# Feed-forward by groups of four output tiles with 512-column matmuls, the left-over sums turned by VectorE and placed by DMAs within SBUF

## What is computed

```python
def conv_ffn(h, buf, w_up, w_gate, conv_w, conv_b, w_down):
    L = h.shape[1]
    up = h @ w_up
    gate = h @ w_gate
    ext = jnp.concatenate([buf.astype(gate.dtype), gate], 1)
    act = jax.nn.gelu(causal_dwconv(ext, conv_w, L) + conv_b)
    return (act * up) @ w_down, ext[:, -(FFN_CONV - 1):]
# in trunk: x = x + y (mixer); x = x + conv_ffn(rms_norm(x), ...); at the end rms_norm(x)
```

## Time and profile before

| | us |
|---|---|
| median of 3 runs (lowest, highest) | 2825.76 (2825.66, 2826.88) |
| profiled execution: device time | 2826.28 |
| profiled execution: span from first to last instruction | 2824.5 |
| TensorE busy | 2805.3 |
| VectorE busy | 1555.3 |
| ScalarE busy | 1032.5 |
| GpSimd busy | 123.6 |

### The profile page before, as it was taken

One profiled execution on the slowest core, in us unless ns is written; L12 is line 12 of the kernel. 1 busy time (PEld: TensorE's weight loads), 2 busy tenths in 40 slices (PEclk: granted clock), 3 DMA queues, 4 the chain that ended last, 5 costly groups with the idle time before them and its releaser, 6 DMA issues.

```text
span 2824.5 us, 49617 instructions
## 1 busy us (share of the span) xinstructions
PE 2805.3 (99%) x19055; PEld 2791.5 (99%) x19055; DVE 1555.3 (55%) x2178; ACT 1032.5 (37%) x1135; POOL 123.6 (4%) x136
## 2 busy tenths in 40 slices
PE   9999999999999999999999999999999999999998
PEld 8999999999999999999999999999999999999998
DVE  7666645554355544555666666455554455535554
ACT  5443333333333333333444444443333333333333
POOL 0000021000000000002200000220000000000012
PEclk9999999999999999999999999999999999999999
DMA  6444344444444444444444444444444444444443
GB/s 237 145 145 137 129 149 149 151 148 151 151 149 144 155 150 149 142 155 149 144 146 151 136 143 142 154 147 151 148 150 149 149 149 149 149 149 149 149 149 114
DMA packets 120784, 420.26 MB, mean 149 GB/s; under 512 B 13688, under 2 KB 19840, under 8 KB 120576
## 3 DMA queue, kind: packets, MB, share of 16 engines
q1 hardware_dynamic: 120128, 418.45, 44.7%
q10 hardware_dynamic: 576, 0.66, 0.1%
HBM read 412.92 MB, written 6.14 MB: 148 GB/s over the span
## 4 chain that ended last, share of the span: by engine, by line
PE 98%; DVE 1%; DMA 0%; ACT 0%; issue 0%; DVEq 0%; ACTq 0%
PE gb L463 95%; PE ab L469 3%; PE ab L482 1%; DMA x<-in_x 0%; DVE w_lo L1097 0%; PE ab L663 0%; DVE work L1731 0%; DVE work L1225 0%; DVE rt L1727 0%; DVE work L1189 0%; ACT w_hi L785 0%; DVE a_lo L1104 0%; DVEq L140 0%; ACT work L862 0%; ACTq L850 0%
## 5 line engine op out<-in xcount | busy, mean ns | idle before, releaser
L1097 DVE TENSOR_TENSOR w_lo<-raw,w_hi 128x1024 fp32r<-128x1024 f32 x767 | 943.4, 1230 | 1175.5 <-ACT w_hi L785 1173.5
L785 ACT ACTIVATE w_hi<-raw 128x1024 fp32r<-128x1024 f32 x769 | 814.5, 1060 | 1653.8 <-PE gb L463 1651.4
L463 PE MATMUL gb<-a_hi,w_hi 128*128 128x320 f32 x4216 | 1311.1, 311 | 0.5 <-DVE w_lo L1097 0.3
L463 PE MATMUL gb<-a_hi,w_lo 128*128 128x320 f32 x4216 | 1302.8, 309 | 0.0
L463 PE MATMUL gb<-a_lo,w_hi 128*128 128x320 f32 x4216 | 1302.7, 309 | 0.0
L463 PEld LDWEIGHTS gb<-a_hi,w_hi 128*128 128x128 f32 x4216 | 791.6, 188 | 2.2 <-DVE w_lo L1097 0.6
L463 PEld LDWEIGHTS gb<-a_lo,w_hi 128*128 128x128 f32 x4216 | 791.6, 188 | 1.2
L463 PEld LDWEIGHTS gb<-a_hi,w_lo 128*128 128x128 f32 x4216 | 791.3, 188 | 0.0
L463 PE MATMUL gb<-b_hi,w_hi 128*128 128x320 f32 x1920 | 593.7, 309 | 0.0
L463 PE MATMUL gb<-b_hi,w_lo 128*128 128x320 f32 x1920 | 593.3, 309 | 0.0
L463 PE MATMUL gb<-b_lo,w_hi 128*128 128x320 f32 x1920 | 593.3, 309 | 0.0
(11 more groups left out here) (182 smaller groups left out, 804.6 us busy)
## 6 DMA issues: line engine op xcount, KB each, us to landing
raw<-in_weights SPq DMA_DIRECT2D x769, 512.0 KB, 3.3
out_y<-work SPq DMA_DIRECT2D x4, 640.0 KB, 3.0
out_c<-work SPq DMA_DIRECT2D x8, 257.0 KB, 5.6
x<-in_x SPq DMA_DIRECT2D x3, 640.0 KB, 7.8
work<-m_scratch SPq DMA_DIRECT2D x8, 192.0 KB, 4.9
work<-in_ret_tables SPq DMA_DIRECT2D x8, 160.0 KB, 3.3
work<-in_ml_state SPq DMA_DIRECT2D x8, 128.5 KB, 5.2
work<-in_w_pool SPq DMA_DIRECT2D x1, 1024.0 KB, 8.5
```

The lines of the kernel that those rows point to most:

```text
L463: last = nc.tensor.matmul(bank(b, m), w[:, at:at + P], v[:, t:t + T], start=kg == k == n == 0, stop=kg == groups - 1 and k == UK - 1 and n ...
L785: nc.scalar.activation(w_hi[:, at:at + UW], raw[:, at:at + UW], ACT.Copy).then_inc(hi_ready, 1)
L1097: V.tensor_tensor(w_lo[:, at:at + UW], raw[:, at:at + UW], w_hi[:, at:at + UW].bitcast(F32), ALU.subtract).then_inc(lo_ready, 1)
```

## The change

In the feed-forward alone the matmuls are cut otherwise. High and low part of an activation tile now lie side by side (a and b, with 640 columns per tile: 320 high, 320 low). A group is now four output tiles (two pairs, all four banks of gb) instead of a pair, and its units come in twos with the same k-tiles (gate and up of the same pair of width tiles; two pairs of the down projection), which the host arranges. Such a quad is worked by wide_quad:

- high_weights: w_hi by 512 columns, the 320 high and the first 192 low (WIDE_LO) ones; columns 320 to 511 of a bank gather the low part's products of tokens 0 to 191;
- low_weights: w_lo by the 320 high columns, as before;
- left_of: the last 128 low columns become the weights, and w_hi of all four output tiles the 512 moving columns; the result, with tokens on partitions, gathers in bank 1 of ab.

Each quad's left_of is issued in the quad before (next_left), and the order of high and low weights changes from quad to quad. When left_of is complete (left_summed) VectorE turns its 32 x 32 blocks into left (turn_left), SyncE issues 16 DMAs of 32 partitions x 128 elements from left to left_t (place_left), and VectorE adds left_t, scaled, to the low sums (ffn_up) or to x (left_to_x). The 192 low columns are added by instructions of their own. ffn_gate (scaling) is now apart from ffn_conv, and GELU and product come one group later in the lists. The last group of all works its last quad pair by pair (apart).

The other projections keep the three matmuls of 320 columns with the new places of a and b.

```diff
+WIDE_LO = 512 - T
-        a_hi, a_lo = sb("a_hi", KT * T, F32R), sb("a_lo", KT * T, F32R)
-        b_hi, b_lo = sb("b_hi", KT * T, F32R), sb("b_lo", KT * T, F32R)
+        a, b = sb("a", KT * 2 * T, F32R), sb("b", KT * 2 * T, F32R)
...
+            def place_left(group):
+                sp.wait_ge(left_turned, group + 1)
+                for tokens in range(4):
+                    for feats in range(4):
+                        sp.dma_start(left_t[feats * 32:(feats + 1) * 32, tokens * P:(tokens + 1) * P],
+                                     left[tokens * 32:(tokens + 1) * 32, feats * P:(feats + 1) * P])\
+                            .then_inc(left_placed[feats], 16)
+            def ffn(unit0, pair0, group):
+                for f, k, u0, p0, down_u, down_p in ffn_blocks(unit0, pair0):
+                    with sp.Fori(0, k // 2) as i:
+                        for j in range(8):
+                            load(Unit(u0 + RING + j, i, 8))
+                        place_left(i + group)
...
+            def left_of(u, q, quads, act):
+                for k in range(UK):
+                    t = (q * UK + k) * 2 * T + T + WIDE_LO
+                    w = w_hi[:, u.slot * UW:(u.slot + 2) * UW].rearrange("p (u k c) -> p u k c", u=2, k=UK)
+                    last = nc.tensor.matmul(left_bank, act[:, t:t + P], w[:, :, k, :], start=q == k == 0,
+                                            stop=q == quads - 1 and k == UK - 1)
+                return last
+            def wide_quad(u, q, quads, act, taken, group, apart=False, fresh=None):
+                final, low_first = q == quads - 1, q % 2 == 1
+                if q == 0:
+                    if fresh is not None:
+                        pe.wait_ge(fresh[0], fresh[1] + 2)
+                    pe.wait_ge(hi_ready, u.number(2))
+                    pe.wait_ge(left_turned, group)
+                    left_of(u, 0, quads, act)
+                def next_left():
+                    if final:
+                        return
+                    if fresh is not None:
+                        pe.wait_ge(fresh[0], fresh[1] + 2 * q + 4)
+                    pe.wait_ge(hi_ready, u.number(4))
+                    last = left_of(u.plus(2), q + 1, quads, act)
+                    if q + 1 == quads - 1:
+                        last.then_inc(left_summed, 1)
+                def high_weights(p):
+                    if q == 0:
+                        pe.wait_ge(pair_taken, taken + p)
...
+                            last = nc.tensor.matmul(gb[:, 2 * p + m, :], w_hi[:, at:at + P], act[:, t:t + 512],
...
+                if low_first:
+                    for p in range(2):
+                        low_weights(p)
+                late = fresh is not None and q == quads - 2
+                high_weights(0)
+                if not late:
+                    next_left()
+                high_weights(1)
+                if late:
+                    next_left()
+                if not low_first:
+                    for p in range(2):
+                        low_weights(p)
...
                         for j in range(8):
                             split(Unit(u0 + AHEAD + 8 + j, i, 8))
                             if j == 1:
+                                ffn_gelu(i + g)
+                            if j == 2:
                                 ffn_upper(i + g, i * 2)
-                            if j == 6:
-                                ffn_gelu(i + (g + 1))
...
+            def turn_left(group):
+                dve.wait_ge(left_summed, group + 1)
+                left_there(group)
+                V.transpose(left_out, ab[:, 1, :].rearrange("p (m b t) -> p m b t", m=4, b=4)).then_inc(left_turned, 1)
+            def left_to_x(group, p):
+                left_there(group + 1)
...
+                V.tensor_tensor(at, at, left_in, ALU.add).then_inc(left_added, 1)
+                dve.wait_ge(left_added, group + 1)
+            def add_wide_to_x(p, b, units, taken):
+                own()
+                used(units)
+                step.inc(V.tensor_tensor(two(tiles(x, p * 2)), banks(b), two(tiles(x, p * 2)), ALU.add))
+                own()
+                V.tensor_tensor(two(tiles(x, p * 2))[:, :, 0:WIDE_LO], lows_of(b),
+                                two(tiles(x, p * 2))[:, :, 0:WIDE_LO], ALU.add).then_inc(pair_taken, 1)
+                dve.wait_ge(pair_taken, taken)
...
+            def ffn_up(units, group, u):
                 used(units)
+                r, ext, s0 = both(rt[:]), two(g_ext, GE), 2 + SEQ + 2
+                V.tensor_tensor(two(low_up)[:, :, 0:WIDE_LO], lows_of(1), r[:, :, 0:WIDE_LO], ALU.mult)
+                V.tensor_tensor(two(up), banks(1), r, ALU.mult).then_inc(pair_taken, 1)
+                split(u)
+                split(u.plus(1))
+                left_there(group + 1)
...
+                    .then_inc(left_added, 1)
+                dve.wait_ge(left_added, group + 1)
+                lo = two(low_gate)
+                V.tensor_tensor(ext[:, :, 2:2 + SEQ], ext[:, :, 2:2 + SEQ], lo[:, :, 0:SEQ], ALU.add)
+                V.tensor_tensor(ext[:, :, s0:GE], ext[:, :, s0:GE], lo[:, :, SEQ:T], ALU.add).then_inc(gate_scaled, 1)
+                step.inc(V.tensor_tensor(up, up, low_up, ALU.add))
...
+                        with counted(dve, 3, [(step, 2)]) as i:
+                            for j in range(8):
+                                if j == 0:
+                                    add_wide_to_x(i * 2 + 1, 1, i * 8 + (down_u + 8), i * 2 + (down_p + 2))
+                                    split(Unit(down_u + AHEAD + 6, i, 8))
+                                    split(Unit(down_u + AHEAD + 7, i, 8))
+                                if j == 7:
+                                    left_to_x(i + (group + 1), i * 2 + 2)
+                                    add_wide_to_x(i * 2 + 2, 0, i * 8 + (down_u + 15), i * 2 + (down_p + 3))
+                                    continue
+                                if j == 5:
+                                    turn_left(i + (group + 1))
+                                if j != 6:
+                                    split(Unit(down_u + AHEAD + 8 + j, i, 8))
```

## The result

The changed kernel takes 2976.16 us (median; lowest 2974.89, highest 2978.91), the kernel before 2826.0 us beside it: a ratio of 1.0531, 95% interval 1.0515 to 1.0547. It is 150 us slower. The forecast was 47 us slower, and 2976 lies above its range. The profiled execution has a span of 2973.4 us, 148.9 more than before.

The account below looks back on a forecast made before the run. TensorE's matmul stream, busy 99% of the span, was taken as the bound. Against 2826.28 us the terms -42 + 32 + 33 + 15 + 2 + 8 were summed to +47, 2873 us, range 2812 to 2906 us.

Parts of the forecast that it names:

- Part 1: Feed-forward matmul stream: fewer, wider matmuls, a quad 6.88 us instead of 7.04, gain 42 us over 264 quads.
- proportional: Rival: the 13.3 ns per matmul beyond the columns grow with width; nothing gained, +73, 2899 us; chance 0.17.
- free at 512: Rival: the 13.3 ns per matmul vanish at 512 columns; gain 106 us, sum +7, 2833 us; chance 0.12.
- Part 2: Left-over sums' way back in down groups: TensorE waits for pair_taken, 32 us in four-quad and 33 us in three-quad groups.
- 0.37 to 0.47; I take 0.47: Step pricing SyncE's issue of each placing DMA, in us; 15 issues before the last one come to 7.05 us.
- X: Time from the turn's end until all 16 placing DMAs have landed: 9.0 us, bounds 7.2 and 10.3.
- 16 four-quad groups: Down groups of four quads: TensorE waits 1.5 us each, 3.3 in the 4 first ones; 32 us in all.
- 7 three-quad waits: Down groups of three quads: TensorE waits 3.9 us each, 2.7 more in the 2 first ones; 33 us.
- Part 3: VectorE's and ScalarE's order in gate/up groups: GELU ahead of a split, TensorE waits 0.35 us in 42 groups, 15 us.
- Something dearer: Rival: the DMAs or the turn cost far more; turn at 3.4 us gives +65, 2938 us; chance 0.10.
- Part 4: Single places: next layer's start 2 us; the end, where the last placing and adds come late, 7.7 us.
- placing in time: Rival: issues 0.37 us apart, landing 1.6, X 7.2; sum -8, 2818 us; chance 0.16, of which 0.09 at 2818.

Follow-up runs that it names:

- The kernel with the waits removed: Changed kernel with all adds in the next group's second step, each layer's last group the old way, GELU behind the split: 2791.63 us, ratio 0.9877.
- The reading from HBM: Changed kernel with the same 16 placing DMAs reading the first weight unit in HBM instead of the turned sums in SBUF: 2878.27 us.
- the run with four DMAs: Changed kernel with only 4 of each group's 16 placing DMAs issued, three quarters of the left-over sums not added: 2802.38 us.

## Why the prediction was right on the side and wrong on the size

**Part 1, right.** The forecast was 226.7 ns for 512 columns, 13.3 of them fixed. Measured starts are 227 or 226 ns apart; 320 columns keep 146.7. The rivals proportional (235) and free at 512 (215) are out. The 215.8 ns of the Trainium skill (TensorE: Matmul & The Clock Gate, Back-to-back issue gap) don't hold for this stream; the page gives that formula for a single matmul by itself, and of a stream with weight loads it says that the formula counts too much at large widths, where here it counts 11 ns too little. The 100 us that the prediction reckoned by it took the formula at 512 columns and the row at 320; the formula at both widths would give 12 x 2.5 ns a quad, 8 us. The kernel with the waits removed shows most of the gain of 42 us: 2791.63, 34 below the kernel before.

**Part 2, the mechanism right, two terms wrong.** TensorE waits for pair_taken behind left_to_x, in the groups named, through the chain named. The turn measured 0.72 for 0.69 and the landing of 16 KB 1.8 for 1.9. The step that failed is "0.37 to 0.47; I take 0.47": it carried the pace of loads from HBM and of a store to it over to issues with both ends in SBUF, and bounded it from above by the same rows. It is 0.63, outside the bounds, and so is X; 15 x 0.16 = 2.4 us per group, X = 11.5 and not 9.0, and with 24 groups 58 us. The reading from HBM gave back 66 us of waits. The 2.0 us of the Trainium skill (DMA: Bandwidth & Descriptors, Anatomy of one DMA) are given there for DMAs that GpSimd issues; from SyncE a landing took 1.8 here. By kind, the waits are:

| | forecast | measured (distances between starts, less the matmul's own time) |
|---|---|---|
| 16 four-quad groups | 32 | 71 |
| 7 three-quad waits | 33 | 46 |
| the end | 8 | 11 |

Where one group is followed through, the forecast with the right X holds: 1.5 + 2.5 for the longer placing - 0.3 for faster adds (2.3 from 731.86 to 734.16, forecast 2.7) is 3.7, and the distance from the end of the left-over product (729.30 + 0.91) to 734.16 is 3.95.

**The missing term.** Nothing in the sum stood for the granted clock. "So every ns of the matmul stream is time, and any new wait of TensorE is time too" counted a wait once; behind these waits it costs about 50.1 / 24 = 2.1 us more. The earlier trace rows could not show it, since the kernel before never waits there and stays at 1.00; but a forecast of 23 new waits had to ask what the clock does behind an idle TensorE, and at least bound it. With both terms, 2873 + 58 + 50 = 2981 us would have been the forecast, against 2976; that is reckoned afterwards, from what was measured.

**Part 3, right.** A wait for w_hi was forecast in 42 groups at 0.35 us, 15 us in all; the profile has 38 and 12.4 us, and taking GELU out of the way gives 9.3 us. "Something dearer" among the rivals named the DMAs, at 2938 us, but priced it by the turn, which was as cheap as expected.

**Part 4, nearly right.** The end cost 11 us for 8, by the same longer placing. The next layer's start was set at 2 us, beside a wait of 6.8 us of the last three-quad group there, which the sum has among its 7.

The rival placing in time (2818) described what the kernel would be with a short X; the run with four DMAs, whose X is shorter still, came to 2802. The issue pace of 0.37, on which this rival rests, lies on the wrong side of what was measured. The terms of the sum, as printed, add up to 48 and not 47; nothing hangs on it.

## What to carry to other kernels

Price a DMA's issue by a row with the same memories at both ends, and where many small DMAs stand in a chain, count issues first: here they were 9.4 of 11.5 us. Let a result that comes late by DMA be added behind the release of what the busiest engine waits for, and not ahead of it; the same DMAs cost some 175 us in one place of VectorE's list and nothing that shows in the next step. And give every new wait of TensorE of some microseconds two prices, its length and the half clock behind it.

## What was not expected of the hardware

- In a row of issues, one of a DMA from SBUF to SBUF keeps the issuing engine's queue for 590 to 601 ns, one from HBM to SBUF with the same shape for 421 ns; 32 rows of 512 B or 128 rows of 128 B make hardly a difference. Stores from SBUF to HBM, by themselves, took 355 ns. Seven weight loads from HBM that SyncE issued right behind a row within SBUF took 580 ns, against 333 by themselves, so part of the price falls on the issue behind. A row of stores to HBM was not tried.
- SyncE and ScalarE issue at the same time nearly without slowing each other (eight in 5.0 and in 5.3 us); ScalarE's activations wait meanwhile.
- At waits of TensorE of 3.9 to 10.6 us the granted clock was at half for 3.4 to 10.2 us, beginning some microseconds behind the start of the wait; at those of 1.2 to 2.2 us in the kernel reading from HBM it stayed at full, and of three of 2.5 us there it fell at two. Why the half-clock stretch at two equal waits of 3.9 us is 3.4 us in one place and 6.8 in another was not tried and stays open.
